# Decoder layer on one core: value ring 4 to 3 tiles, row ring 7 to 8, set-up reordered

## The reference

```python
proj = h @ w_in                                   # attention q/k/v, recurrence, memory q, gates
a_out = dilated_attention(dil, rel_bias)          # 3 groups x 4 heads, relative bias table
b_out = hgrn2(f_raw, i_in, q_in, g_in, lb, norm)  # gated recurrence
k, v = split(mem @ w_mem_kv)                      # 256 memory tokens, 4 heads
c_out = softmax(q_mem @ k.T) @ v
h = LN(alpha*h + sum(sigmoid(gate_b) * (branch_b @ w_branch_b)) @ w_out)
# expert layer: per token 8 heads x top 16 of 16384 experts -> 128 picks
act = gelu(einsum('td,ted->te', h, u_tab[idx]))
ffn = einsum('te,ted->td', gate * act, v_tab[idx])
h = LN(alpha*h + ffn)
```

## Time and profile before

| | us |
|---|---|
| median of 3 runs | 3980.63 |
| the three runs | 3977.09, 3980.63, 3981.24 |
| the profiled execution, its own time | 3969.75 |
| its span, first to last instruction | 3967.9 |
| PE busy | 3624.0 (91%) |
| DVE busy | 2817.0 (71%) |
| POOL busy | 1577.5 (40%) |
| ACT busy | 1320.5 (33%) |

### The profile page before, as it was taken

The page is one execution under the profiler, slowest core; times in us unless marked ns, Lnnn a source line. Parts: engine busy times, 40 slices in busy tenths (PEclk is TensorE's granted clock), DMA queues, the critical chain, the costliest instruction groups (busy, mean ns, idle before and its releaser), DMA issues.

```text
span 3967.9 us, 47017 instructions
## 1 busy us (share of the span) xinstructions
PE 3624.0 (91%) x14687; PEld 2482.4 (63%) x14687; DVE 2817.0 (71%) x5664; ACT 1320.5 (33%) x2671; POOL 1577.5 (40%) x1341
## 2 busy tenths in 40 slices
PE   6999999999988989877879998998998999999997
PEld 5787878777777768655444553554544545558874
DVE  1455542248778876657989888888888868868777
ACT  1333342222333232225251330421412404228345
POOL 1565544331222257655353444444444444520000
PEclk8999999989999999988999999999999999999999
DMA  6676633346777768868999999999999999984667
GB/s 236 207 233 217 216 120 95 109 152 238 250 240 236 243 204 262 286 239 305 334 409 395 400 391 383 389 375 386 407 375 369 409 402 393 394 322 144 209 213 245
DMA packets 506335, 1134.06 MB, mean 286 GB/s; under 512 B 41180, under 2 KB 250508, under 8 KB 505904
## 3 DMA queue, kind: packets, MB, share of 16 engines
q1 hardware_dynamic: 335120, 570.94, 41.3%
q0 software_dynamic: 147456, 536.94, 36.0%
q10 hardware_dynamic: 23584, 24.12, 1.8%
HBM read 1044.81 MB, written 89.41 MB: 286 GB/s over the span
## 4 chain that ended last, share of the span: by engine, by line
PE 33%; DVE 12%; DMA 6%; issue 2%; ACT 0%; POOL 0%; DVEq 0%; ACTq 0%; SPq 0%
PE ps L1427 22%; PE ps L1460 7%; DVE u_ring L2448 5%; PE ps L1413 4%; DMA u_ring<-in_peer_u,pidx 3%; DMA v_ring<-in_peer_v 2%; DVE hot L2440 1%; DVE hot L2441 1%; DMA score_in<-subkeys_t 1%; DVE split_v L2501 1%; DVE got_own L2047 0%; DVE inds_own L1990 0%; DVE inds_own L2002 0%; DVE left_own L1993 0%; ACT split_v L1889 0%
## 5 line engine op out<-in xcount | busy, mean ns | idle before, releaser
L1427 PE MATMUL ps<-v_ring,table 128*128 128x512 f32 x3072 | 1362.5, 594 | 11.5 <-DMA v_ring<-in_peer_v 11.3
L1023 POOL DMA_INDIRECT u_ring<-in_peer_u,pidx x800 | 773.7, 967 | 929.7 <-DVE coefe L2448 861.8
L2448 DVE CUSTOM_DVE_ANT_0 u_ring<-u_ring,h_up 128x1024 f32<-128x1024 f32 x800 | 947.3, 1215 | 136.6 <-DMA u_ring<-in_peer_u,pidx 118.4
L1427 PEld LDWEIGHTS ps<-v_ring,table 128*128 128x128 f32 x3072 | 568.9, 191 | 655.1 <-issue 629.0
L1084 PE MATMUL ps<-x_hi,w_hi 128*128 128x512 f32 x1280 | 514.0, 402 | 22.5 <-ACT w_hi L1537 15.1
L1087 PE MATMUL ps<-x_lo,w_hi 128*128 128x512 f32 x1280 | 504.3, 394 | 0.0
L1460 PE MATMUL ps<-split_v,split_c 128*128 128x512 f32 x1536 | 372.6, 396 | 21.9 <-DVE split_v L2501 19.1
L1413 PEld LDWEIGHTS ps<-hot,hot 128*128 128x128 f32 x2048 | 280.9, 202 | 148.0 <-issue 94.4
L988 POOL DMA_INDIRECT e_ring<-in_peer_u,icole x224 | 228.5, 1020 | 345.6 <-DVE dotse L2101 266.4
L967 POOL TENSOR_TENSOR w_lo<-w_raw,w_hi 128x1024 fp32r<-128x1024 f32 x120 | 300.9, 2513 | 159.8 <-ACT w_hi L1537 153.8
L1858 ACT ACTIVATE table<-ps 128x512 f32<-128x512 f32 (+3 forms) x256 | 230.5, 901 | 374.4 <-PE ps L1413 331.9
(11 more groups left out here) (327 smaller groups left out, 4412.5 us busy)
## 6 DMA issues: line engine op xcount, KB each, us to landing
v_ring<-in_peer_v SPq DMA_DIRECT2D x576, 512.0 KB
w_raw<-in_w_in SPq DMA_DIRECT2D x88, 512.0 KB
wh_d<-w_hi SPq DMA_DIRECT2D x56, 512.0 KB, 2.6
wl_d<-w_lo SPq DMA_DIRECT2D x56, 512.0 KB, 4.0
w_hi<-wh_d SPq DMA_DIRECT2D x56, 512.0 KB
w_lo<-wl_d SPq DMA_DIRECT2D x56, 512.0 KB, 4.9
u_ring<-in_peer_u,pidx POOLq DMA_INDIRECT x800
raw_mid<-in_w_branch SPq DMA_DIRECT2D x48, 256.0 KB
```

The costliest lines, as they stand in the source:

```text
L1023: pool.indirect_dma_start(out=u_ring[:, slot_of(n, k), :], out_offset=None, in_=u_tab, in_offset=bass.IndirectOffsetOnAxis(ap=pidx[n % 2][ ...
L1427: last = pe.matmul(ps[2 * (n % 2) + c][:, :], table[:, row_of(n, i1), :], v_ring[:, j % V_TILES, HALF * c:HALF * c + HALF], start=(n == p ...
L2448: dve.tensor_tensor_reduce(out=u_ring[:, slot_of(n, k), :], in0=u_ring[:, slot_of(n, k), :], in1=h1_up[:, :, :].rearrange("p c n -> p (c n)"),
```

## The change

The value ring loses a tile and the row ring gains one. In the set-up, the loads are issued in another order, and each group has a semaphore of its own; the closed half of the bias table has a tile of its own (`closed_bias`), so that DVE's overwrite in the middle of the table's writes and the barrier behind it are gone; PE's order is memory transposes, memory keys, sub-key transposes, x transposes, memory values; the first two tiles of `w_in` are loaded ahead of the waits for the table; and SP waits for all of the set-up's writes before the first read of the bias table (`k0`, weight tile 5) instead of before the first weight tile. One barrier (the first) is gone. In pass 0 SP loads the second block's inputs ahead of value tile 3 instead of 4.

```diff
-U_ROWS = 7
-V_TILES = 4
+U_ROWS = 8
+V_TILES = 3
...
-            sp.dma_start(sk_n[:, :, :], A["peer_sub_keys"]...).then_inc(setup_in, 16)
-            sp.dma_start(mem_n[:, :, :], A["mem"]...).then_inc(setup_in, 16)
-            sp.dma_start(wkv[:, :, :], w_kv[:, :, 0:HALF]).then_inc(kv_in, 16)
-            sp.dma_start(wvv[:, :, :], w_kv[:, :, HALF:2 * HALF]).then_inc(kv_in, 16)
-            sp.dma_start(x_n[0][:, :, :], x_d[0, 0:HALF, :]...).then_inc(xn_in, 16)
+            sp.dma_start(mem_n[:, :, :], A["mem"]...).then_inc(mem_in, 16)
+            sp.dma_start(wkv[:, :, :], w_kv[:, :, 0:HALF]).then_inc(wk_in, 16)
 
             sp.wait_ge(setup_dve, 2)
             sp.dma_start(bias_rows.rearrange("g h y -> h g y"), brow[:, :, :]).then_inc(setup_dma, 16)
+            sp.dma_start(sk_n[:, :, :], A["peer_sub_keys"]...).then_inc(sk_in, 16)
+            sp.dma_start(x_n[0][:, :, :], x_d[0, 0:HALF, :]...).then_inc(xn_in, 16)
             sp.wait_ge(setup_dma, 16)
...
             sp.dma_start(bias_skew, rep).then_inc(setup_dma, 16)
+            sp.dma_start(wvv[:, :, :], w_kv[:, :, HALF:2 * HALF]).then_inc(wv_in, 16)
+            for n in range(2):
+                c0 = HEAD_TILES[n][1]
+                sp.dma_start(w_raw[n][:, :, :], w_in[:, :, c0:c0 + P]).then_inc(w_landed[n], 16)
             sp.wait_ge(setup_dma, 32)
...
             sp.dma_start(bias_tabs[1].rearrange("a p k -> p a k"), tab[:, :, :]).then_inc(setup_dma, 16)
-            sp.wait_ge(setup_dma, 16 * n + 16)
-            sp.sem_inc(bias_out, 1)
-            sp.wait_ge(setup_dve, 9)
-            sp.dma_start(bias_tabs[0].rearrange("a p k -> p a k"), tab[:, :, :]).then_inc(setup_dma, 16)
-            sp.wait_ge(setup_act, 24)
+            sp.dma_start(bias_tabs[0, :, :, P:2 * P]..., tab[:, :, P:2 * P]).then_inc(setup_dma, 16)
+            sp.dma_start(bias_tabs[0, :, :, 0:P]..., closed_bias[:, :]...).then_inc(setup_dma, 16)
+            sp.wait_ge(setup_act, 30)
             sp.dma_start(subkeys_t, sk_t[:, :, :]).then_inc(setup_dma, 16)
-            sp.wait_ge(setup_dma, SETUP_DMAS)
...
-                sp.wait_ge(stage, 3 * (boundary(0, 0) - 1))
                 for h in range(NH):
                     for t, (name, c0) in enumerate(HEAD_TILES):
                         n = NT_HEAD * h + t
+                        if n < 2:
+                            continue
+                        if h == 0 and name == "k0":
+                            sp.wait_ge(setup_dma, SETUP_DMAS)
+                            sp.wait_ge(stage, 3 * boundary(0, 0))
                         if name[0] == "k":
                             edges(0, h, h, int(name[1]))
...
-                    if p == 0 and i == 4:
+                    if p == 0 and i == 3:
...
+            dve.memset(closed_bias[:, :], NEG)
             dve.memset(tab[:, 2 * NH:3 * NH, :], NEG).then_inc(setup_dve, 1)
...
-            dve.wait_ge(bias_out, 1)
-            dve.memset(tab[:, :, 0:P], NEG).then_inc(setup_dve, 1)
-            dve.wait_ge(setup_dve, 9)
-            dve.sem_inc(setup_dve, 1)
-            cross(dve, 1)
```

More of the change, by code:

```diff
@@ L396, in layer @@
         rows36 = at("rows36", [36, P])
-        tab = at("tab", [P, G * NH, 2 * P])
         relb = at("relb", [BUCKETS, G * NH])
         sk_n = at("sk_n", [P, 2 * PH, P])
-        sk_t = at("sk_t", [P, 2 * PH, P])
+        sk_t = at("sk_t", [P, 2 * PH, P], offset=where["bias"])
         mem_n = at("mem_n", [P, 2, D])
@@ L403, in layer @@
         wkv = at("wkv", [P, KD, HALF])
-        wvv = over("wvv", "x_hi", [P, KD, HALF])
-        x_n = [at("x_n0", [P, NB, D], offset=r_side), at("x_n1", [P, NB, D], offset=r_top)]
+        x_n = [at("x_n0", [P, NB, D])]
+        assert top[0] <= r_side
+        tab = at("tab", [P, G * NH, 2 * P], offset=r_side)
+        closed_bias = at("closed_bias", [P, P])
+        assert top[0] <= where["idxo"]
+        wvv = over("wvv", "branch", [P, KD, HALF])
+        x_n.append(at("x_n1", [P, NB, D], offset=r_top))
         table = at("table", [P, ROWS, P], offset=r_c)
@@ L1042, in _, with transposes, transposed_half @@
                           start=True, stop=True).then_inc(setup_pe, 1)
-            pe.wait_ge(setup_in, 32)
+            def transposes(out, blocks):
+                for n, src in enumerate(blocks):
+                    last = pe.transpose(out[:, P * n:P * n + P], src, ident[:, :])
+                return last
+            def transposed_half(src, it):
+                for k in range(KD):
+                    if it == 0 and k == 2:
+                        pe.wait_ge(setup_act, 30)
+                    if k >= 4:
+                        pe.wait_ge(XV.sem, XV.after(f"lo{k - 4}", it))
+                    transposes(ps[turn_bank(k, it)], [src[:, tb, P * k:P * k + P] for tb in range(NB)]).then_inc(*XP.mark(f"t{k}"))
+            pe.wait_ge(mem_in, 16)
             for q in range(4):
@@ L1047, in _ @@
                     pe.wait_ge(setup_act, 20 + q - 1)
[L1048 to L1059, removed]
+                transposes(ps[6 + q % 2], [mem_n[:, j % 2, P * (2 * q + j // 2):P * (2 * q + j // 2) + P] for j in range(4)]).then_inc(setup_pe, 1)
+            pe.wait_ge(setup_act, 24)
             pe.wait_ge(setup_dve, 1)
-            pe.wait_ge(kv_in, 32)
+            pe.wait_ge(wk_in, 16)
             for h in range(NH):
@@ L1096, in tile @@
                 return last
-            def transposes(out, blocks):
-                for n, src in enumerate(blocks):
-                    last = pe.transpose(out[:, P * n:P * n + P], src, ident[:, :])
-                return last
             def turned_rows(hf, it):
@@ L1114, in turned_rows @@
                     transposes(ps[turn_bank(k, it)], [res[:, tb, P * k:P * k + P] for tb in range(NB)]).then_inc(*XP.mark(f"t{k}"))
-            def transposed_half(src, it):
-                for k in range(KD):
-                    if k >= 4:
-                        pe.wait_ge(XV.sem, XV.after(f"lo{k - 4}", it))
-                    transposes(ps[turn_bank(k, it)], [src[:, tb, P * k:P * k + P] for tb in range(NB)]).then_inc(*XP.mark(f"t{k}"))
             def early_scores(q):
```

67 lines of the change are left out of this document (37 added, 30 removed).

## The result

The changed kernel takes 4021.3 us, the median of three runs (4015.5 to 4022.1; a fourth took 5369 us at a granted clock of 0.65 and is left out), beside 3978.9 us for the kernel before in the same session (3974.0 to 3981.2, four runs). The ratio is 1.0111 with a 95% interval of 1.0096 to 1.0126: slower by 44 us (38 to 50). I had forecast +14, 3995 us, in a range of 3968 to 4024. It is in the range and in the direction, but the loss is three times what I took.

What follows compares the result with a forecast made beforehand. It took PE and DMA together as the limit in the full part and value slots in the last pass; -17 + 30 + 0 + 5 - 4 = +14 us gave 3995 us, range 3968 to 4024.

Steps and rivals of the forecast that it cites:

- Step 4: Three value slots in the full part, where transfers fill the chip: +5 us, between 0 and +15.
- Rival C: First halves of passes: PE starves for values, loads staying 8.3 us; +80 less 40 at turns, sum +54, 4035 us; chance 0.12.
- the turns: Ends of passes, where PE waits for the last dots: these waits would still be some 60 us in all.
- Step 2: Three value slots in the last pass, taken as bound by slots: +30 us, between +20 and +40.
- Rival B: Last pass: a load is mostly queue, shrinking to 3.9 us with three slots; +14 there, sum -2, 3979 us; chance 0.16.
- Step 3: Three value slots in passes 6 and 7: 0 us, the loads still hidden behind PE's work.
- Step 5: Eight row slots, one more row in after each search: -4 us, between 0 and -10.
- rival A: Row gathers limited by latency, so eight row slots cure the turns: -35 us, sum -17, 3964 us; chance 0.12.
- Step 1: Set-up before the first projection, reordered loads and fewer waits: -17 us, between -20 and -8.
- Rival D: Set-up gives nothing, weights or `wvv` late behind the table's transfers: sum +31, 4012 us; chance within the forecast's 0.60.
- the 20 loads: Last pass: SP's 20 value tile loads between two stores would take 50 us instead of 39.5.
- the nines: Full part: the profile's slices of DMA busy share would stay at 9.

Runs made afterwards that it cites:

- e5: Kernel before, four value slots kept, but SP issues loads as if there were three in passes 0 to 6: 4008.5 us, ratio 1.0080.
- e6: Kernel before, SP issuing value loads as if there were three slots in pass 0 alone: 3985.6 us, ratio 1.0034.
- e7: Kernel before, with three value loads in flight from tile 36 of pass 6 on: 4005.9 us, ratio 1.0088.
- e1: Kernel before with old set-up and only the new ring sizes (8 row slots, 3 value slots): 4033.2 us, ratio 1.0144.
- e2: Kernel before with old set-up, 3 value slots and still 7 row slots: 4028.4 us, ratio 1.0145.
- e4: e3 with four set-up writes (three of the table, one of the sub-keys) moved behind the third and fourth weight tile: 3966.4 us, ratio 0.9978.
- e3: Changed kernel with the old rings (7 row slots, 4 value slots), so the new set-up alone against the kernel before: 3969.2 us, ratio 0.9981.
- e9: Kernel before with six value slots in the last pass, two laid over the dead one-hot buffers: 3953.7 us, ratio 0.9947.
- e8: e2 (3 value slots, 7 row slots) with only five row gathers in flight: 4044.2 us, ratio 1.0172 against the kernel before.

## Why the prediction was right or wrong

**Step 4, three slots in the full part: wrong, and it is the miss.** It stood at +5 and cost +28 to +34 by waits and marks, +32 when timed alone (e5). The sentence that failed is "With one or two in flight it should be some 5 to 6". With three slots the loads that PE waits for take 6.4 to 9.4 us in pass 0, and the median of all loads from 2110 to 3400 is 6.9 us, the same as with four slots (e6). I had worked out 8.3 us from the earlier trace rows and found it "three times 2.56: a queue, not a latency". That argument is empty. The 2.56 us are not PE's pace: PE works 1.98 us on a tile and then stands idle for a value load, in these very rows. Where a ring of four slots sets the pace, a load is four times the pace less the 1.98 us of work, and that is some three times the pace whatever the load is made of. The two tiles that cover a load are 4.0 us in pass 0 and 6.9 in passes 1 to 6. Pass 0 had no price at all in the prediction, although show PE waiting there with four slots; it cost 13.5 us (e6). The place at tile 48 was foreseen: 15.63 us of load, PE's wait up to 6.2.

**Rival C had the wait right, its price by luck.** That loads do not get short with a slot less is what happened, though at a median of 6.9 and not 8.3 us. Its +80, less 40 at the turns, was for the first halves of passes 1 to 6. From 2110 to 3600 the waits for values rose by 29.3 us (1.7 to 31.0), and those at the turns fell by 20.8 (52.0 to 31.2). The other half of the new waits, 32.4 us, is in pass 0, of which C says nothing; and the 10.8 us of its turn went. That C's net 40 comes near the measured 32 is two errors that meet. Its sum of +54 (4035) is 10 too high. I gave it 0.12, arguing that with four slots PE lost almost nothing: that shows that a load fits three tiles, not that it fits two, and in pass 0 it was not even so.

**Step 2, the last pass: right in mechanism, a little too dear.** +30 forecast, +23 to +24 by the marks of three kernels (e7 alone was timed at +35, 29 to 41). The term that was off is the load with three slots: 4.7 taken, 4.14 measured, 0.06 under my lower bound. That bound came from a row with two loads issued together. The rule of the Trainium skill (DMA: Bandwidth & Descriptors, Anatomy of one DMA) that I weighed there gives 3.2 us for a tile. With two slots 3.4 was measured, so it is close for a nearly idle queue, but its outcome here, that nothing is lost, is refuted. Rival B is half right: the load shrinks from 5.16 to 4.14 with one slot fewer, where I had worked out 3.9. It fails on its tail of "+14" against 24 and on the full part.

**Step 3, passes 6 and 7 at nothing: right.** The shift is +28.4 at tile 44 of pass 6 and +27.5 at that of pass 7.

**Step 5, the eighth row: -4 forecast, 0 measured** (e1 and e2 have the same ratio), and rival A falls with it. DMA was full, as the rows said.

**Step 1, the set-up: the first projection right, the end not.** -17 forecast and -19.3 at the first projection. But I had called the table's writes "hidden", and said what the loss of that cover would do: hold back the loads of weights behind them. It did, by 5.37 us at the third tile: the skewed copy took 19.6 us and not the 13 I had taken over from before, SP was through with the writes only near 64, and the tile's load waited for them. The 2 us for a better clock did not come at once either: in the 20 us behind the first projection the granted clock was 0.91, before 0.90. A reordering by two tiles only shifts this (e4). Of the 12 us left halfway about 7.5 reach the end (e3). Where the last 5 went was not settled; it is within what identical code varies between programs. Rival D, that the set-up gives nothing because loads come late behind the table's transfers, is half right: of the 17 us 7.5 reach the end, and the 5.37 at the third tile are lost for this reason.

**The sum.** Measured: -7.5 + 28 to 34 + 24 + 0 = +44 to +50, against +44 (38 to 50) for the whole. Against the forecast, step 4 is off by +23 to +29, step 1 by +9.5, step 2 by -6 and step 5 by +4. That 4021 is inside the range is no merit of the forecast: its bound of +15 for step 4 was passed twice over. The bounds that I had, -10 and +47, give 3971 to 4028, not the 3985 beside the chances, and the full slices of the earlier trace rows are sixteen, not fourteen. Of what I said the profile would show, the set-up (59 for 63 us), the 20 loads (45.8 for 50), the DMA share at the end (0.66 for 0.6), ACT's longer wait for values there (53.4 us for 39.2 in windows of 123 us) and the nines came; the turns did not stay at 60 but fell to 31. And PE's waits for values in passes 1 to 6 passed 20 us, at 31.0, which I had named as the sign of C.

## What to carry to other kernels

Price a ring slot in each stage by itself: the load's duration under that stage's own traffic, plus the hold, against the number of slots times the pace of a tile. A stage that hides its loads with n slots says nothing about n - 1, and a load time worked out from the pace of a ring holds only where the user is seen waiting for each landing. That it is nearly as many paces as there are slots then follows from the ring, and says nothing about a queue. Look for buffers that are dead in the stage where the ring is the limit: the two slots borrowed in e9 brought 21 us, where a ring one slot shorter in all stages lost 57 (e1).

## What the runs showed of the hardware that was not expected

- A 512 KB load from SP, beside row gathers that keep the DMA share at 0.98 to 1.0, takes a median of 6.9 us with three value slots and with four; with five row gathers in flight instead of seven or eight it is 6.7. Those that PE waits for have a mean of 8.07 us in e2 and in e8 (1960 to 3600, a few long ones behind other loads included).
- On the less busy chip of the last pass the same load takes 3.4, 4.14 and 5.16 us with two, three and four slots, at 172, 209 and 252 GB/s.
- Two weight loads that SP issues while the skewed copy is under way occupy SP itself for 10.93 us, and the 2 MB load of `wvv` ahead of them for 7.90, where a load is mostly issued in 0.4 to 0.9 us: the issue is held back, and with it everything behind it on SP. Here it ended as the copy landed (38.6).
- The skewed copy took 13.2 us at a DMA share of 0.52 and 19.6 us at 0.97.
